# Modulation vectors with output features on partitions: one multiply-and-sum on VectorE for each tile of 128 features

## The reference

```
def adaln_params(cond, w, b):
    mod = jax.nn.silu(cond) @ w + b          # (1024) @ (1024, 6144) + (6144)
    return jnp.split(mod[..., None, :], 6, axis=-1)

sh1, sc1, g1, sh2, sc2, g2 = adaln_params(c, mod_w[i], mod_b[i])
h_lat = modulate(rmsnorm(x, norm_g[i, 0]), sh1, sc1)
x = x + g1 * hyena_mix(h_lat, p)
x = x + g2 * conv_ffn(modulate(rmsnorm(x, norm_g[i, 1]), sh2, sc2), *ffn_p, rows, GRID_W)
return rmsnorm(x, final_g)
```

## Time and profile before

| | us |
|---|---|
| median of 3 runs (1061.87 to 1062.69) | 1061.96 |
| the profiled execution, its own time | 1061.37 |
| its span in the trace | 1059.3 |
| PE busy (share) | 1040.0 (98%) |
| DVE busy | 665.7 (63%) |
| POOL busy | 543.7 (51%) |
| ACT busy | 418.6 (40%) |
| PE, share of the chain that ended last | 95% |

### The profile page before, as it was taken

How to read it: one execution, slowest core, us unless ns; L and a number is a source line. 1 busy time by engine, 2 the same in 40 slices (tenths; PEclk the granted TensorE clock), 3 DMA queues, 4 the chain that set the end, 5 groups by cost and what they waited for, 6 DMA issues and landing times.

```text
span 1059.3 us, 13471 instructions
## 1 busy us (share of the span) xinstructions
PE 1040.0 (98%) x4968; PEld 856.4 (81%) x4968; DVE 665.7 (63%) x1007; ACT 418.6 (40%) x687; POOL 543.7 (51%) x401
## 2 busy tenths in 40 slices
PE   7999999999999999999999999999999999999996
PEld 5889887877877888778888888778888888888885
DVE  5663776866499765985788847386666666520503
ACT  6223547665554243644444342442323223221222
POOL 1688895999200064234444346535465545553641
PEclk9999999999999999999999999999999999999999
DMA  6446454342446922212322113303222232223222
GB/s 257 164 168 225 133 187 153 90 163 70 179 159 238 379 104 100 93 67 80 110 83 84 54 42 155 143 33 146 87 80 79 103 135 79 80 80 135 104 80 79
DMA packets 19611, 131.92 MB, mean 125 GB/s; under 512 B 3411, under 2 KB 3811, under 8 KB 13030
## 3 DMA queue, kind: packets, MB, share of 16 engines
q1 hardware_dynamic: 8784, 92.62, 23.2%
q0 software_dynamic: 6560, 27.27, 8.0%
q10 hardware_dynamic: 4214, 11.30, 2.8%
HBM read 124.90 MB, written 6.30 MB: 124 GB/s over the span
## 4 chain that ended last, share of the span: by engine, by line
PE 95%; DVE 2%; ACT 1%; DMA 1%; issue 0%; POOL 0%; SPq 0%; POOLq 0%; ACTq 0%; DVEq 0%
PE bank L505 81%; PE bank L496 7%; PE bank L511 3%; PE bank L752 1%; PE bank L746 1%; DMA x_sb<-x_in 1%; PE bank L904 1%; PE bank L741 1%; DVE arena L2178 0%; DVE arena L2181 0%; PE bank L913 0%; PE bank L753 0%; PE bank L869 0%; ACT arena L1189 0%; DVE arena L2214 0%
## 5 line engine op out<-in xcount | busy, mean ns | idle before, releaser
L1730 POOL TENSOR_TENSOR ring_parts<-ring,ring_parts 128x1024 fp32r<-128x1024 f32 x102 | 248.7, 2442 | 266.3 <-ACT ring_parts L1189 263.5
L505 PE MATMUL bank<-hT_parts,ring_parts 128*128 128x512 f32 x1344 | 339.2, 393 | 0.8 <-ACT hT_parts L1518 0.8
L1189 ACT ACTIVATE ring_parts<-ring 128x1024 fp32r<-128x1024 f32 (+2 forms) x163 | 168.6, 1043 | 383.7 <-PE bank L505 219.9
L505 PEld LDWEIGHTS bank<-hT_parts,ring_parts 128*128 128x128 f32 x1344 | 249.6, 188 | 54.7 <-ACT hT_parts L1518 2.4
L505 PE MATMUL bank<-ring_parts,hT_parts 128*128 128x512 f32 (+1 forms) x672 | 171.6, 379 | 1.0 <-POOL ring_parts L1730 0.6
L505 PE MATMUL bank<-ring_parts,arena_parts 128*128 128x512 f32 (+1 forms) x736 | 172.4, 386 | 0.0
L505 PEld LDWEIGHTS bank<-ring_parts,arena_parts 128*128 128x128 f32 x736 | 136.6, 188 | 27.9 <-DVE arena L2416 0.3
L505 PE MATMUL bank<-arena_parts,ring_parts 128*128 128x512 f32 x592 | 148.0, 391 | 0.3 <-DVE arena_parts L2285 0.3
L505 PEld LDWEIGHTS bank<-ring_parts,hT_parts 128*128 128x128 f32 x672 | 122.4, 188 | 22.8 <-POOL ring_parts L1730 1.0
L2521 DVE SCALAR_TENSOR_TENSOR arena<-bank,small,arena 128x441 f32<-128x441 f32 (+2 forms) x176 | 122.3, 695 | 24.6 <-DVE arena L2521 1.7
L505 PEld LDWEIGHTS bank<-arena_parts,ring_parts 128*128 128x128 f32 x592 | 111.0, 188 | 25.4 <-DVE arena_parts L2285 2.1
(11 more groups left out here) (223 smaller groups left out, 1100.5 us busy)
## 6 DMA issues: line engine op xcount, KB each, us to landing
ring<-weights_in SPq DMA_DIRECT2D x39, 2048.0 KB, 8.0
arena<-mod_w_in POOLq DMA_DIRECT2D x32, 512.0 KB, 4.1
arena<-mod_w_in POOLq DMA_DIRECT2D x8, 1024.0 KB, 5.5
x_sb<-x_in SPq DMA_DIRECT2D x4, 512.0 KB, 5.7
ring<-weights_in SPq DMA_DIRECT2D x4, 512.0 KB, 8.5
mod_spill<-mod_part POOLq DMA_DIRECT2D x16, 128.0 KB, 2.1
x_sb<-x_in ACTq DMA_DIRECT2D x4, 512.0 KB, 12.2
arena<-mod_spill ACTq DMA_DIRECT2D x1, 2048.0 KB, 10.6
```

The lines of the kernel that those rows point to most:

```text
L505: ins = nc.tensor.matmul(out, l, r, start=start and n == 0, stop=stop and n == len(passes) - 1)
L1189: return nc.scalar.activation(out, in_, ACT.Copy)
L1730: return nc.gpsimd.tensor_tensor(part(low), low, part(high), ALU.subtract)
```

## The change

- The weights are re-laid with *output* features on partitions: 48 tiles of 128 outputs by 1024 inputs (512 KB). silu(c) is needed as a row on all partitions (`cond_row`, half of `mod_g`): POOL loads it, ACT applies Silu to 128x1024.
- One DVE operation for each tile (`mod_tile`) multiplies the tile by `cond_row` and sums along the free axis into one column of `modc`.
- 16 tiles go before attention, beside the rotations and the splits of pieces 12 to 23, with three buffers; 32 go beside the gate and projection pieces, with four buffers. POOL only issues the loads, each with a wait for the tile that used its buffer; `latent_roots` stands behind `load_mod(10)`.
- POOL's 32 rounds of multiply and add, its 16 spills, the spill's load, DVE's 64 operations on 256 outputs, PE's `modulation` and `gate_rows`, and the copies out of their banks are gone.
- The bias is added once for all 48 columns behind the merge. The gates go as 2048 single values to DRAM and come back as rows on all partitions (two more DMAs on ACT's queue). The tables for the transforms are loaded earlier.

The diff, cut to its core:

```diff
+MOD_TILES = 6 * KD
+MOD_EARLY = 16
...
+        cond_row = mod_g[:, 0, :]
+        modw_early = [at(99, D), at(103, D), mod_g[:, 1, :]]
+        modw_late = [at(75, D), at(79, D), at(65, D), at(69, D)]
@@ PE
-            modulation(0)
-            gate_rows(0)
             wo_tile(0)
             wo_tile(1)
-            modulation(1)
-            gate_rows(1)
             filter_tile(0)
             wo_tile(2)
-            modulation(2)
             filter_tile(1)
...
             wo_tile(7)
-            gate_rows(2)
-            gate_rows(3)
-            modulation(3)
@@ ACT
             for p in range(4, 15):
                 split_high(p)
+                if p == 8:
+                    wait("cond_in", 16)
+                    nc.scalar.activation(cond_row, cond_row, ACT.Silu).then_inc(sem("cond_ready"), 1)
...
-            wait("mod_pool_done", MOD_POOL)
...
             square_x2(TT - 1)
+            wait("gates_ready", 1)
+            act.dma_start(mod_row_d.rearrange("a (t p) -> p (a t)", p=P), modc[:, 4 * KD:MOD_TILES],
+                          allow_slow_non_contiguous=True).then_inc(sem("mod_row_out"), 16)
...
+            wait("mod_row_out", 16)
+            act.dma_start(mod_g[:].rearrange("p a b -> p (a b)"),
+                          mod_row_d.partition_broadcast(P).rearrange("p a d -> p (a d)")).then_inc(sem("modg_in"), 16)
@@ POOL
+            def load_mod(j):
+                if j < MOD_EARLY:
+                    b, buffers, name = j % len(modw_early), modw_early, "modw_early"
+                    used = j - len(modw_early) + 1
+                else:
+                    b, buffers, name = (j - MOD_EARLY) % len(modw_late), modw_late, "modw_late"
+                    used = j - len(modw_late) + 1 if j >= MOD_EARLY + len(modw_late) else 0
+                if used > 0:
+                    wait("mod_summed", used)
+                pool.dma_start(buffers[b], mod_d[:, j * D:(j + 1) * D]).then_inc(sem(f"{name}{b}"), 16)
...
+            chunk_landed(pool, C_DK)
+            pool.dma_start(cond_row, cond_d.partition_broadcast(P).rearrange("p a d -> p (a d)")).then_inc(sem("cond_in"), 16)
+            for j in range(MOD_EARLY):
+                load_mod(j)
+                if j == 10:
                     latent_roots()
+            for h in range(HEADS):
+                head_roots(h)
+            wait("o_ready", HEADS)
+            load_mod(MOD_EARLY)
+            load_mod(MOD_EARLY + 1)
+            wait("pv_done", 4 * UNITS)
+            for j in range(MOD_EARLY + 2, MOD_TILES):
+                load_mod(j)
@@ DVE
+            def mod_tile(j):
...
+                V.scalar_tensor_tensor(out=w, in0=w, scalar=1.0, in1=cond_row, op0=ALU.mult, op1=ALU.mult,
+                                       accum_out=modc[:, j:j + 1]).then_inc(sem("mod_summed"), 1)
...
                 rope_tile(roped[i // 4][:, i % 4, :], in_bank(i), i % 4, 8).then_inc(sem("rope_out"), 1)
                 split_low(8 + i)
+                if i == 3:
+                    wait("cond_ready", 1)
+                if i >= 4:
+                    mod_tile(i - 4)
-            for p in range(16, 24):
+            for p in range(16, 20):
                 split_low(p)
+                mod_tile(p - 12)
+            for p in range(20, 24):
+                split_low(p)
+                for j in range(2):
+                    mod_tile(8 + 2 * (p - 20) + j)
...
             for p in range(FIRST_GATE + 6, FIRST_PD + 4):
                 split_low(p)
+                for j in range(2):
+                    mod_tile(MOD_EARLY + 2 * (p - FIRST_GATE - 6) + j)
                 if p in (FIRST_GATE + 8, FIRST_GATE + 9):
                     split_output(p - FIRST_GATE + UNITS - 10)
                 if p - FIRST_GATE - 7 in NET_AFTER:
                     net_layer(NET_AFTER.index(p - FIRST_GATE - 7))
-                if p - FIRST_GATE in MOD_AFTER:
-                    mod_chunk(MOD_AFTER.index(p - FIRST_GATE))
...
             split_low(FIRST_WO + 2)
             split_low(FIRST_WO + 3)
+            modulation()
...
             norm_x2(2)
-            modg_late(2)
             norm_x2(3)
-            modulation()
             scale_n2(2)
-            modg_late(3)
             add_abs(6)
             scale_n2(3)
```

More of the change, by code:

```diff
@@ L892, in _ @@
                          [(o[0][:, k, :], o[1][:, k, :]) for k in range(HEADS)]).then_inc(sem("merge_done"), 1)
[L895 to L914, removed]
             def abs_norm(n):
@@ L1418, in _ @@
                 split_high(p)
+            wait("mod_summed", MOD_TILES)
+            act.dma_start(at(75, 1024), tables_d[:, 0:1024]).then_inc(sem("tables_in"), 16)
             def wout_split(n):
@@ L1452, in abs_out @@
                     nc.scalar.activation(abs_tap(i, d), taps(d, n)[:, t, :], ACT.Abs).then_inc(sem("abs_ready"), 1)
-            def modg_copy(j):
-                wait("modg_done", j + 1)
-                copy(mod_g[:, 0, j * 512:j * 512 + 512], bank[MODG_BANK[j]]).then_inc(sem("modg_out"), 1)
             def square_x1(m):
@@ L1951, in net_layer @@
                 wrap(r, a, k, 0).then_inc(sem("net_angle"), 1)
-            def mod_chunk(j):
-                C = MOD_DVE_COLS
-                wait(f"modw_in{j % 2}", 16 * (MOD_POOL // 2 + j // 2 + 1))
-                acc = mod_g[:].rearrange("p a b -> p (a b)")[:, j * C:(j + 1) * C]
-                w = modw_dve[j % 2]
-                for k in range(KD):
-                    ins = V.scalar_tensor_tensor(out=acc, in0=w[:, k, :], scalar=st(CSILU + k), in1=acc, op0=ALU.mult, op1=ALU.add)
-                    if k < KD - 1:
-                        link(ins)
-                ins.then_inc(sem("mod_dve_done"), 1)
             def table(t, m, groups, halves):
@@ L2107, in split_output, with modulation @@
                 V.tensor_tensor(part(low), low, part(high), ALU.subtract).then_inc(sem("oT_low"), 1)
+            def modulation():
+                wait("mod_summed", MOD_TILES)
+                V.tensor_tensor(modc[:], modc[:], small[:, SMALL["mod_b"]], ALU.add).then_inc(sem("gates_ready"), 1)
+                wait("gates_ready", 1)
+                for s, name in enumerate(("norm_g1", "norm_g2")):
+                    c = modc[:, (2 * s + 1) * KD:(2 * s + 2) * KD]
+                    ins = V.scalar_tensor_tensor(out=c, in0=c, scalar=1.0, in1=small[:, SMALL[name]], op0=ALU.add, op1=ALU.mult)
+                ins.then_inc(sem("modc_ready"), 1)
             wait("lambda_exps", 1)
@@ L2151, in _ @@
                     split_low(FIRST_PD + 4 + d // 2)
+                    mod_tile(MOD_TILES - 4 + d // 2)
             for d in range(KD):
@@ L2160, in _ @@
             split_low(FIRST_WO + 3)
-            def modulation():
-                wait("modc_done", 4)
-                V.tensor_tensor(modc[:], bank[3][:, 0:4 * KD], small[:, SMALL["mod_b"]], ALU.add).then_inc(sem("modc_read"), 1)
-                wait("modc_read", 1)
-                for s, name in enumerate(("norm_g1", "norm_g2")):
-                    c = modc[:, (2 * s + 1) * KD:(2 * s + 2) * KD]
-                    ins = V.scalar_tensor_tensor(out=c, in0=c, scalar=1.0, in1=small[:, SMALL[name]], op0=ALU.add, op1=ALU.mult)
-                ins.then_inc(sem("modc_ready"), 1)
+            modulation()
             def add_abs(i):
```

112 lines of the change are left out of this document (21 added, 91 removed).

## The result

The changed kernel takes 1070.74 us (median of 4 runs, 1070.3 to 1071.79) beside 1062.22 for the kernel before on the same chip: a ratio of 1.0083, 95% interval 1.007 to 1.0095. It is slower by 0.8%, and the time lies outside the range that was given (1058 to 1067). The profiled execution took 1070.3 us and has a span of 1068.5, 9.2 more than before.

What follows compares the result with a forecast made beforehand. PE's own list was taken to bound the kernel (busy 1040.0 of 1059.3 us); 1061.4 - 10.4 removed + 5.0 lost again + 5.9 in the latents + 0.2 at the net = 1062.1, given as 1062.3 us, range 1058.0 to 1067.0.

Steps and rivals of the forecast that it cites:

- The sum: Whole kernel: 1061.4 - 10.4 + 5.0 + 5.9 + 0.2 = 1062.1 us; middle given as 1062.3.
- nothing behind gives it back: Behind the latents: the 5.9 us lost there stays lost, as PE has hardly a wait until 384 us.
- The latents: Beside C_DGATE: load 11 waits behind the roots, PE stands still 4.0 us near 126 us; 5.9 us lost in all.
- Rival 4: PE's stall near 126 us: a rest of 4.0 us lowers the clock, costing 1.7 us, time 1064.0; chance 0.15.
- a fall of the clock behind the wait: Behind PE's wait near 126 us: named as a sign that the forecast is wrong.
- The cost of a tile: DVE's mod_tile, multiply and sum of 1024-wide tensors: taken as 1.3 us, bounds 1.2 and 2.5.
- Rival 3: DVE's mod_tile: the accumulating operation runs at half pace, 2.4 us a tile, time 1078 or worse; chance 0.08.
- The rotations and the net: Last rotation at 81.1 us, just in time; filter net's angle at 300.1 beside the gates, 0.2 us charged, up to 2.
- Behind the merge: From 384 us to the second block's first high_out: of 10.4 us removed 5.0 are lost, a lead of 5.4.
- At the turn itself: First turn of the second block: lead of 5.2 plus 0.6 us for a DVE copy gone; 0.35 charged for ACT's DMA issue.
- Rival 1: Latents: the stall hardly happens, as loads or roots come sooner or the work fits the slack; 1056.3 to 1058.8 us, chance 0.15.

Runs made afterwards that it cites:

- e9: Changed kernel with modc moved behind the arena and 32 unused columns ahead of it, arena at byte 115328 as before the change; 1063.01 us, ratio 1.0003.
- e2: Kernel before with 16 unused columns behind modc, so its arena starts at byte 115392, no instruction differing; 1069.89 us, ratio 1.0072.
- e4: e1 with 16 more PE passes ahead of PE's wait for the low part of piece 22; 1070.28 us.
- e5: Changed kernel, latent_roots behind the last early load, modc behind the arena, 32 unused columns ahead, arena at byte 115328; 1057.32 us, ratio 0.9956.
- e1: Changed kernel with 16 unused columns (64 bytes) behind modc, arena at byte 115456; 1070.92 us.
- e3: e1 with latent_roots behind the last early load instead of behind load 10; 1065.23 us.
- e10: e5 with DVE making the low part of piece WO+2 in its gap ahead of the merge's last tile; 1054.62 us, ratio 0.9928.
- e11: e10 with filter_tile(7) behind wo_tile(7), scale_taps(7) behind add_wo(7), squares of x2 ahead of the DMA issues; 1054.87 us, ratio 0.9937.
- e7: e5 with stat behind the arena and no padding, so the arena starts 512 bytes lower; 1056.67 us.
- e6: e5 with sums behind the arena too, so the arena starts 256 bytes lower; 1056.31 us.
- e8: e5 with 16 unused columns ahead of everything, so ring, hT, x_sb and arena start 64 bytes later; 1055.93 us, ratio 0.9941.

## Why the prediction was wrong, point by point

- **The sum left a part out.** This is the step that failed. Each edit to the engines' lists was priced; the declarations weren't, and 16 more columns of `modc` cost about 7.7 us (1070.7 to 1063.0, e9), more than anything that was priced but the removal itself. The claim that "nothing behind gives it back", and with it the silent one that a pass costs what it did in the trace of before, failed: the changed kernel loses 0.75 us between the latents and the end of the merge, where e9 loses nothing, and 6.0 us from the first turn of the second block to the end (3.23 to 9.2), where e9 loses 0.6 (2.56 to 3.2) with 1.3 of slower clock in it. The kernel before with its arena moved (e2) loses 7.9 with no other change. No row of before shows such a cost; the full diff shows its cause. The kernel pads its tensors to a line of 128 bytes just ahead of the place where the change makes one longer, and that should have been a rival.
- **The rest of the sum came close, in part by luck.** With the place mended the kernel is 0.6 us above the kernel before measured beside it (1063.01 and 1062.45), where the sum gave 0.7. But the ten launches lie between 1061.0 and 1064.3, and the profiled one is 2.9 above the profiled kernel before: it loses 8.0 us in the latents, where 5.9 was forecast, and 1.3 by the clock behind the first turn, which the sum didn't have at all.
- **The latents.** Forecast: load landed at 127.3, split at 129.8, PE still for 4.0 us, first latent product at 145.7. Measured: 128.0, 130.4, 3.86 us, and 147.31 for the first latent product (145.86 in e4). The roots ended 0.7 us later than before, as POOL started them at 121.24 instead of 120.55. PE too came 0.7 us later to piece 22 (126.4 instead of 125.75), of which its passes of 352 columns took 0.6 (last section). So 0.7 of the 1.6 us above the forecast stood at the restart already, and about 0.5 is the clock (e4).
- **Rival 4, the clock in the stall,** came about, at 0.15. The prediction had named a fall of the clock behind the wait as a sign that it was wrong. Its price of 1.7 us was too high all the same: the slow passes lose 2.6 (10.98 against 8.41 us), and only about 0.5 of that reaches the first latent product, as PE would have waited for DVE otherwise. The row that spoke for it deserved more weight than 0.15, with a rest of 4 us forecast.
- **The cost of a tile.** Taken at 1.3 us. The 48 operations of `mod_tile` take 1.218 us (1.208 to 1.226), and the next operation starts 1.14 us after the start; the readout of the sum, 0.08 us, hides in that. Rival 3 falls wholly. Its rule, from the Trainium skill, "Vector Engine (DVE) Microarchitecture Reference", section "Points that are easy to get wrong", halves the throughput of this instruction where both SBUF sources aren't bf16; both are float32 here and nothing is halved.
- **The rotations and the net** didn't hold PE, as forecast. The last rotation ended at 80.67 (forecast 81.1). The net's angle ended at 306.39, which is 298.5 on the scale of before (7.9 us earlier), 1.6 before the 300.1 of the forecast, and PE asks at 308.48 without waiting; the 0.2 charged there was nothing.
- **Behind the merge.** Forecast: 5.4 us of 10.4 are kept. From 384.66 to the first turn the table shows 7.98 - 2.56 = 5.42 us in e9, and 5.07 in the changed kernel, whose passes on the arena are slow there too. The wait at `wo_tile(0)` is 0.81 for DVE and 0.40 for ACT's last part of `sgd`, which wasn't counted. At the turn itself the forecast was a lead of 5.8 us, less 0.35 for ACT's extra DMA issue; that issue takes 0.60 us and costs nothing that the trace shows, since PE waits for the first `high_out` 0.52 us before and 0.51 after. Ahead of the turn it is 0.94 + 1.95 = 2.89 us where nearly 3 was said.
- **Rival 1** could be had, once the place was mended, by an edit of one number (e5): 1057.3, inside its 1056.3 to 1058.8.

## What to carry to other kernels

A change that alters the size of any tensor moves all that is declared behind it; before pricing instructions, compare the addresses, and where PE has long stretches without waits, read the distance from pass to pass in them in both traces. A busy time that rises while instructions fall says the same at a glance. On an engine's queue, ask of every wait what stands behind it: the loads behind two roots cost 5.7 us (e1 less e3), and putting the roots last costs nothing. With the place, this order and the early split mended together, e10 is 0.7% faster than the kernel before.

## What the runs showed of the hardware

**Distance between PE's operands.** A pass of 128x512 whose two operands lie a multiple of 256 bytes apart within a partition takes 0.2266 us from start to start; at 32, 64 and 128 bytes off it takes 0.2289 to 0.2334, depending on which operand is which. With 256 columns nothing of the kind shows: in the latents six passes of 128x256 with the stationary operand in the arena take 0.88 us before and 0.86 in the changed kernel. Distances above 128 that aren't a multiple of 256 weren't tried. Why it is so, the runs don't show.

**A pass of 352 columns varies by execution.** Between 82 and 114 us four and two such passes took 0.95 us from start to start in the profiled executions of the kernel before, e3, e4 and e11, and 0.97 in the other ten. The whole stretch takes 0.6 us longer by it, and e1 has the same addresses as e3 and e4, e10 the same as e11. What decides isn't known.

**The clock behind short rests.** Ten profiled kernels have the same rests ahead of the second block's input: 0.94 to 1.00 us, the spectrum, 1.95 or 1.96 us, a turn. In five (after, e1, e4, e7, e10) the granted clock stays at 1.00 behind them, in five (e3, e5, e6, e8, e9) it falls to 0.50. PE of e5 and of e10 behind the second rest:

```profile
450.76 2.08 PE L495 MATMUL bank<-hT_parts,ring_parts 128*128 128x512 f32 x4 [0.51 <-ACT hT_parts L1475]
```
```profile
449.51 1.20 PE L495 MATMUL bank<-hT_parts,ring_parts 128*128 128x512 f32 x4 [0.51 <-ACT hT_parts L1475]
```

The same four passes, half the clock in one and the full clock in the other. It costs about 1.3 us. It may account for part of the spread of e9: the five slowest of its ten launches (1063.3 to 1064.3) have a mean granted clock of 0.993, the other five (1061.0 to 1062.8) one of 0.995 or 0.996, but only the slowest was traced. The kernel before, whose PE arrives at the turn without a rest, lies between 1061.3 and 1063.4 in its launches beside them, so not all of the spread is this. A rest of 2 us can thus cost more than its own length, in some executions and not in others.
